# The compressed attention branch with both key groups in one TensorE product, padded to 128 rows

## The reference, cut to what matters

```python
s_c = jnp.einsum("bqgrd,bngd->bqgrn", qb, k_cmp) * scale     # n = 31 compressed keys, d = 64
m_c = (cmp_last[None, :] <= t[:, None])[None, :, None, None, :]
p_c, _, _ = _masked_softmax(s_c, m_c)
o_c = jnp.einsum("bqgrn,bngd->bqgrd", p_c.astype(qb.dtype), v_cmp)
...
return gb[..., 0:1] * o_c + gb[..., 1:2] * o_s + gb[..., 2:3] * o_w
```

## Time and profile before

| | before |
|---|---|
| median of 3 runs | 1529.16 us |
| lowest, highest of the 3 | 1528.4, 1537.82 us |
| the profiled execution's own time | 1526.18 us |
| span of the profiled execution | 1524.4 us |
| mean granted TensorE clock | 0.989 of full |
| TensorE matmul busy | 1455.0 us, 95% of the span |
| VectorE, ScalarE, GpSimd busy | 52%, 40%, 37% |

### The profile page before, as it was taken

How to read it: one execution, slowest core, us unless ns; L and a number is a source line. 1 busy time by engine, 2 the same in 40 slices (tenths; PEclk the granted TensorE clock), 3 DMA queues, 4 the chain that set the end, 5 groups by cost and what they waited for, 6 DMA issues and landing times.

```text
span 1524.4 us, 20393 instructions
## 1 busy us (share of the span) xinstructions
PE 1455.0 (95%) x7122; PEld 1140.8 (75%) x7122; DVE 790.8 (52%) x1413; ACT 605.0 (40%) x1104; POOL 569.4 (37%) x236
## 2 busy tenths in 40 slices
PE   6988999999999999789999999999999999999996
PEld 5656878888888888446778888888877777666785
DVE  6885542223444578895452223444477437676434
ACT  5443432232222436764432223222264335644432
POOL 3222354444444343211344444444434642222341
PEclk9999999999999999899999999999999999999998
DMA  5211222222222322100223222222214321111221
GB/s 215 73 56 51 97 97 96 96 96 97 96 96 96 97 84 83 55 29 29 69 83 96 96 96 98 97 96 97 97 66 126 124 97 56 56 56 56 70 69 55
DMA packets 36624, 129.55 MB, mean 85 GB/s; under 512 B 4048, under 2 KB 4176, under 8 KB 36560
## 3 DMA queue, kind: packets, MB, share of 16 engines
q1 hardware_dynamic: 35136, 124.80, 24.6%
q10 hardware_dynamic: 1424, 3.90, 0.7%
HBM read 126.58 MB, written 2.10 MB: 84 GB/s over the span
## 4 chain that ended last, share of the span: by engine, by line
PE 45%; issue 37%; POOL 14%; DVE 3%; ACT 1%; POOLq 0%; DVEq 0%; ACTq 0%
POOL w L627 14%; PE bank L644 13%; PE bank L646 13%; PE bank L645 13%; PE bank L769 2%; PE bank L783 2%; PE bank L749 1%; PE bank L1079 0%; DVE rms L1634 0%; DVE opC L1602 0%; PE bank L713 0%; DVE arena L2172 0%; DVE arena L2051 0%; PE bank L702 0%; DVE arena L1785 0%
## 5 line engine op out<-in xcount | busy, mean ns | idle before, releaser
L627 POOL TENSOR_TENSOR w<-raw,w 128x1024 fp32r<-128x1024 f32 x232 | 569.1, 2457 | 921.9 <-ACT w L1188 543.1
L644 PE MATMUL bank<-opC,w 128*128 128x512 f32 x624 | 253.5, 406 | 15.0 <-DVE opC L1602 10.5
L646 PE MATMUL bank<-opC,w 128*128 128x512 f32 x624 | 245.2, 393 | 0.0
L645 PE MATMUL bank<-opC,w 128*128 128x512 f32 x624 | 244.8, 392 | 0.0
L1761 DVE TENSOR_TENSOR mlp_op<-arena,mlp_op 128x512 fp32r<-128x512 f32 x64 | 144.5, 2260 | 188.7 <-ACT mlp_op L1303 188.7
L1275 ACT ACTIVATE w<-raw 128x1024 fp32r<-128x1024 f32 x126 | 133.2, 1057 | 239.5 <-PE bank L646 239.5
L644 PE MATMUL bank<-mlp_op,w 128*128 128x512 f32 x544 | 212.3, 390 | 3.1 <-ACT arena L1393 1.4
L646 PE MATMUL bank<-mlp_op,w 128*128 128x512 f32 x544 | 211.8, 389 | 0.0
L645 PE MATMUL bank<-mlp_op,w 128*128 128x512 f32 x544 | 211.8, 389 | 0.0
L644 PE MATMUL bank<-opA,w 128*128 128x512 f32 x416 | 162.8, 391 | 2.2 <-DVE arena L1756 1.3
L646 PE MATMUL bank<-opA,w 128*128 128x512 f32 x416 | 162.0, 389 | 0.0
(11 more groups left out here) (218 smaller groups left out, 1922.2 us busy)
## 6 DMA issues: line engine op xcount, KB each, us to landing
raw<-stream_dram SPq DMA_DIRECT2D x232, 512.0 KB, 3.4
out_t_dram<-arena SPq DMA_DIRECT2D x8, 256.0 KB, 2.2
x<-x_t_dram SPq DMA_DIRECT2D x4, 256.0 KB, 5.7
x<-x_t_dram ACTq DMA_DIRECT2D x4, 256.0 KB, 7.0
rope<-ropes_dram ACTq DMA_DIRECT2D x2, 512.0 KB, 6.8
con<-consts_dram ACTq DMA_DIRECT2D x1, 993.5 KB, 8.2
arena<-p_t_dram ACTq DMA_DIRECT2D x1, 512.0 KB, 3.7
par<-params_dram ACTq DMA_DIRECT2D x1, 253.5 KB, 3.8
```

The lines of the kernel that those rows point to most:

```text
L627: pool.tensor_tensor(w_lo[:, j, :], raw[:, j, :], w_hi[:, j, :].bitcast(F32), ALU.subtract).then_inc(lo_made, 1)
L644: pe.matmul(out, wh, hi, start=first, stop=False)
L645: pe.matmul(out, wh, lo, start=False, stop=False)
L646: return pe.matmul(out, wl, hi, start=False, stop=last)
```

## The change

For a compressed pair all three TensorE steps now treat both key groups at once.

- Scores: `cmpk` becomes 128 x 64 with the keys of group 0 in rows 0 to 63, columns 0 to 31, those of group 1 in rows 64 to 127, columns 32 to 63, and zeros elsewhere. One product with the whole 128 x 128 query tile gives 128 x 64 scores, both groups side by side in one PSUM bank. The 32nd column is now computed too and masked.
- Turn: the probabilities of both groups lie side by side in one buffer and are transposed at once into 64 rows. ScalarE copies them with one instruction in place of two.
- Values: `cmpv` becomes 128 x 128, with values of group 0 in rows 0 to 31, columns 0 to 63, of group 1 in rows 32 to 63, columns 64 to 127, and zeros elsewhere. One product contracts over 128 rows; the rows 64 to 127 of the moving operand hold what an earlier unit left there, and meet zeros.
- Preparation: two memsets on VectorE ahead of the last attention; `compressed` issues the value product twice, once per row block; the eviction takes four instructions in place of two.

```diff
-        cmpk = sb("cmpk", [P, 32])
-        cmpv = sb("cmpv", [32, P])
+        cmpk = sb("cmpk", [P, 64])
+        cmpv = sb("cmpv", [P, P])
...
-                n = N_CMP if br == 0 else P * (qt + 1)
+                n = 32 if br == 0 else P * (qt + 1)
...
+                q = z2(8 + u["r"])[:, P * qt:P * (qt + 1)]
+                return dict(qk=[(q, cmpk[:, :]) if br == 0 else (q[b, :], z2(11 + 2 * br)[b, 0:n])], n=n, both=br == 0,
...
-                            v=[cmpv[0:N_CMP, b]] if br == 0 else
+                            v=[cmpv[:, :]] if br == 0 else
...
+        def scores_of(units, i):
+            n = units[i]["n"]
+            return bank[2][:, n * (i % 2):n * (i % 2 + 1)] if both(units, i) else bank[2 + i % 2][:, 0:n]
+        def shares_of(units, i):
+            n = units[i]["n"]
+            return probs(i - i % 2, SEQ)[:, n * (i % 2):n * (i % 2 + 1)] if both(units, i) else probs(i, n)
...
+                    if both(units, 2 * p):
+                        pe.matmul(bank[2][:, 0:2 * units[2 * p]["n"]], *units[2 * p]["qk"][0], start=True,
+                                  stop=True).then_inc(s_full, 2)
+                        return
...
+                    if both(units, i):
+                        at, u = units[i]["out"][1], units[i]
+                        pe.matmul(into[:, at:at + P], u["v"][0], tmp[:, 4, 0:P], start=u["first"], stop=u["last"],
+                                  skip_group_check=True).then_inc(pv_done, 2)
+                        return
...
+                    if both(units, 2 * p):
+                        w = 2 * units[2 * p]["n"]
+                        pe.transpose(bank[4][0:w, 0:P], probs(2 * p, w), ident).then_inc(pt_full, 2)
+                        return
...
-                return pe.matmul(into[0:32, P:2 * P], hid[:, 1, :], g("w2v", 0, P), start=True, stop=True)
+                for at in (0, 32):
+                    mm = pe.matmul(into[at:at + 32, P:2 * P], hid[:, 1, :], g("w2v", 0, P), start=True, stop=True)
+                return mm
...
+                        if both(units, i):
+                            if i % 2 == 0:
+                                m = 2 * u["n"]
+                                nc.scalar.activation(tmp[0:m, 4, 0:P], bank[4][0:m, 0:P], ACT.Copy).then_inc(pt_ready, 2)
+                            continue
...
-                    mark(TS(cmpk[:, :], src[:, 0:32], 0.5, None, ALU.mult))
-                    TS(cmpv[:, :], src[0:32, P:2 * P], 0.5, None, ALU.mult).then_inc(z_ready, 1)
+                    mark(TS(cmpk[0:64, 0:32], src[0:64, 0:32], 0.5, None, ALU.mult))
+                    mark(TS(cmpk[64:P, 32:64], src[64:P, 0:32], 0.5, None, ALU.mult))
+                    mark(TS(cmpv[0:32, 0:64], src[0:32, P:P + 64], 0.5, None, ALU.mult))
+                    TS(cmpv[32:64, 64:P], src[32:64, P + 64:2 * P], 0.5, None, ALU.mult).then_inc(z_ready, 1)
...
+            mark(nc.vector.memset(cmpk[:, :], 0.0))
+            step(nc.vector.memset(cmpv[:, :], 0.0))
             attention("last", last_out, behind=behind_last)
```

More of the change, by code:

```diff
@@ L557, in unit @@
                 qt, br = u["qt"], u["branch"]
-                n = N_CMP if br == 0 else P * (qt + 1)
+                n = 32 if br == 0 else P * (qt + 1)
                 col = 32 * qt + 9 * u["g"] + 3 * u["r"] + br
-                return dict(qk=[(z2(8 + u["r"])[b, P * qt:P * (qt + 1)],
-                                 cmpk[b, 0:N_CMP] if br == 0 else z2(11 + 2 * br)[b, 0:n])], n=n,
-                            mask=c("cmpmask", 32 * qt, 32 * qt + N_CMP) if br == 0 else c("causal", 640 - n, 640),
+                q = z2(8 + u["r"])[:, P * qt:P * (qt + 1)]
+                return dict(qk=[(q, cmpk[:, :]) if br == 0 else (q[b, :], z2(11 + 2 * br)[b, 0:n])], n=n, both=br == 0,
+                            mask=c("cmpmask", 32 * qt, 32 * (qt + 1)) if br == 0 else c("causal", 640 - n, 640),
                             scale=HD ** -0.5, sink=None,
-                            v=[cmpv[0:N_CMP, b]] if br == 0 else
+                            v=[cmpv[:, :]] if br == 0 else
                               [z2(12 + 2 * br)[:, P * t + b.start:P * t + b.stop] for t in range(qt + 1)],
@@ L578, in program, with both @@
         GROUP0 = {"even": 0, "mla": 4}
+        def both(units, i):
+            return units[i].get("both", False)
+        def scores_of(units, i):
[4 more added lines that the diff above has]
+            return probs(i - i % 2, SEQ)[:, n * (i % 2):n * (i % 2 + 1)] if both(units, i) else probs(i, n)
         def out_bank(family, group):
@@ L1235, in exponentials @@
                         w = u["n"] + (u["sink"] is not None)
-                        nc.scalar.activation(probs(i, w), tmp[:, i % 2, 0:w], ACT.Exp, bias=negm[:, i:i + 1], scale=-1.0,
+                        nc.scalar.activation(shares_of(units, i) if both(units, i) else probs(i, w), tmp[:, i % 2, 0:w], ACT.Exp, bias=negm[:, i:i + 1], scale=-1.0,
                                              accum_out=den[:, i:i + 1]).then_inc(exp_done, 1)
@@ L1712, in reductions @@
                         nc.vector.tensor_tensor_reduce(
-                            tmp[:, i % 2, 0:u["n"]], bank[2 + i % 2][:, 0:u["n"]], u["mask"], -u["scale"],
+                            tmp[:, i % 2, 0:u["n"]], scores_of(units, i), u["mask"], -u["scale"],
                             3e38 if u["sink"] is None else col, ALU.add, ALU.min, negm[:, i:i + 1]).then_inc(masked, 1)
@@ L1723, in shares @@
                         dve.wait_ge(vstep, inverted[i % 2])
-                        pr = probs(i, u["n"])
+                        pr = shares_of(units, i)
                         if u["gate"] is None:
```

## The result

The change makes the kernel slower by 0.17%: 1531.47 us median (20 runs, 1528.8 to 1533.54) against 1528.46 (20 runs of the kernel before beside them), ratio 1.0017, 95% interval 1.0009 to 1.0025. The forecast was 1524.5 us, 0.3% faster, and its range ended at 1529.5. The profiled execution took 1529.27 us against 1526.18, with a mean granted clock of 0.985 against 0.989.

What follows compares the result with a forecast made beforehand. TensorE was taken as the bound, its matmuls covering 95% of the span. Scores and values 3.85 plus turn 1.1 less 0.3 added work gave 4.65 us off 1529.16: 1524.5 us; own range 1522.3 to 1526.2, overall 1521 to 1529.5.

Steps and rivals of the forecast that it cites:

- Scores and values: TensorE's compressed blocks in the last attention: ten records become six, 1.07 to 0.67 us each, 3.85 us saved in all.
- turn: Two 31-column transposes on TensorE become one of 64 columns: 11 x 0.10 = 1.1 us saved, alternatives 0 or 2.3.
- Rival (a): In padded TensorE records weights no longer load beside a matmul, 0.3 us more per block: 1527.3 us, chance 0.04.
- Absorbed blocks: Blocks of steps 24 and 39 only lengthen TensorE's waits in steps 25 and 40, so their 0.40 us each gives nothing.
- What it adds: Extra value product of `compressed` (0.15 us) and two more eviction pieces (0.17) lose 0.3 us, bounds 0.1 and 0.6; memsets hidden.
- Less work for ScalarE (12 copies): ScalarE's 12 fewer copies, like the extra softmax column, lie beside TensorE's stream and count 0.
- (b): The longer wait of step 25 makes TensorE's clock fall, costing 1.7 us: 1526.2 us, chance 0.11.
- (d): The clock falls from step 25 for 10.24 us, costing 5.1 us, slower than before: 1529.6 us, chance 0.04.
- (c): More TensorE waits on VectorE and ScalarE open, taking back four of eight blocks, 1.6 us: 1526.1 us, chance 0.13.

Runs made afterwards that it cites:

- e3: e1 with VectorE evacuating each dilated group's values ahead of the step's other work, not behind it: 1519.7 us, ratio 0.994.
- e1: The changed kernel, with ScalarE skipping the two leftover waits of a compressed pair's second unit: 1528.66 us, ratio 1.0004.
- e2: The kernel before with one more, long-met wait on ScalarE ahead of its wait for the sum of the exponentials: 1531.67 us, ratio 1.003.
- e5: The kernel before with VectorE evacuating each dilated group's values ahead of the step's other work: 1525.05 us, ratio 0.9978.
- e9: e1 with TensorE's filling products ahead of the values in steps 25, 35, 40 and 45: 1527.04 us, ratio 0.998.
- e4: The kernel before with the compressed keys and values evicted in four pieces in place of two, layout unchanged: 1530.19 us, ratio 1.0016.
- e6: The kernel before with only the compressed pairs' scores in one padded product, turns and values still in pieces: 1530.01 us, ratio 1.0004.
- e7: e1 with the padding for turn and values alone, scores made in two pieces as before: 1529.32 us, ratio 1.0.
- e10: e9 with VectorE also evacuating each dilated group's values ahead of the step's other work: 1521.25 us, ratio 0.9947; again 1520.21 us, 0.995.

## Why the prediction was wrong

**Scores and values, turn: right.** 0.66 us a block against 0.67, 0.11 a turn against 0.10. Within the block some luck: the scores take 0.16 and the values 0.28, where the sum had 0.22 for each. The term for both was 4.95 us; from step 12 to the normalisation e3 gains 4.83, net of a wait of step 25 that grew by 0.29 and one of step 40 that grew by 0.41. Rival (a) is refuted: two value records with 128 rows take 0.28 us up to the start of the turns, and the six records of the block 0.66, not 0.3 more. The rule of the Trainium skill (TensorE: Matmul & The Clock Gate, Part 3), that a load overlaps a running matmul only when the row group differs, doesn't hold for these records either: the six take 0.11 us each. The 64-column turn pays no pause, as the row of 31 columns had said; of the term's bounds, 0 and 2.3, neither came. The restriction in the Trainium skill, TensorEngine Tiling (Array Packing), Restrictions and Gotchas, that column tiling excludes the transpose mode for 32-bit input, fits the trace: the next product starts 0.05 us behind the 64-column turn.

**Absorbed blocks: about right.** The waits of steps 25 and 40 grew by 0.29 (e1) and 0.40 us, where I had 0.40 each.

**What it adds: 0.3 forecast, 0.65 measured.** The extra product of `compressed` costs TensorE nothing: its four records took 0.41 us (line 1069), as two did. The eviction was priced by two pieces' mean; it took 0.63 us more on VectorE, twice my upper bound of 0.30, and none of that was hidden. Nor were the memsets, held to be hidden, quite free (0.12 us at V4). The bound for the term, 0.6, was just passed.

**"Less work for ScalarE (12 copies), lie beside TensorE's stream: 0" failed.** I counted the instructions ScalarE loses and not the waits that stay behind when they go. One of them moved a table load of 1.28 us from under VectorE's work onto the path of step 25. It is worth 1.35 us by itself; with the half clock, the kernel before pays 3.0 us for it (e2). The view that would have shown it beforehand is ScalarE's timeline behind the copies: a load that is free only as long as no wait comes ahead of it.

**The clock, put at nothing in the forecast, failed as well, and the rivals (b) and (d) in their size and place.** I let the clock fall at one place, step 25, for 1.7 us or 5.1, from the point at which its idle piece reaches the 2.45 us of step 7; 0.15 for both together. The runs show it behind pieces of 1.89 (e5), 2.18 (e1) and 1.18 us and a second short wait behind it (step 40 of the changed kernel), at up to three places, 13.65 us of half clock in all. (d) had the right sign, at 1529.6, by luck: half of the clock's loss lies elsewhere, and the wait of step 25 was opened by the table load, not by the block. (c) didn't come: no wait but those of steps 25, 40 and 45 grew in e3. And the steps 35, 40 and 45 had no rival at all, although two of them were in my rows as waits.

**The account of the changed kernel**, from its marks and e3's: blocks and turns -5.6 us (the 4.83 of e3 and the 0.29, 0.41 and 0.07 by which its waits of steps 25, 40 and 45 grew); memsets and eviction +0.6; the longer wait of step 25 +1.65, of which the table load is 1.35; half clock behind it +2.7; behind steps 40 and 45 +1.7 and +1.6; longer waits of steps 40 and 45 +0.5: +3.15 us, against 3.16 measured. Without the bare wait the rest is about even with before (e1), and without the half clock the sum would be a gain, so it took both for the loss.

**The range.** Its own terms give 1525.9 us as the upper end of the forecast (1524.5 + 1.1 + 0.3), not 1526.2; the result lies above either.

**Open**: what decides whether an idle piece of about 2 us draws a stretch at half clock. The same piece of step 7, 2.45 us, did in before and did not in e9; that of step 25 with 2.18 us did in e1 and did not in e3, and with 1.89 us it did in e5 and did not in before and e4. Plainest is step 35: its two pieces, 1.38 or 1.39 and 0.56 us, are the same in before, after and e1 to e7, and a stretch at half clock follows in e1, e6 and e7 alone. What the traces show to differ is the place in time: 1315.48 (e1) and 1309.97 (e3) for the end of the piece in step 25. So a part of e3's gain, too, may be its place. An eviction in whole 128-row pieces, and the early evacuation with the bare wait left in, weren't tried.

## What to carry to other kernels

When an instruction is dropped and its waits are kept, look at what the orphaned wait now stands ahead of: here it cost 1.35 us by pushing a table load behind another engine's work. On an engine that is 95% busy a local gain can be forecast to a hundredth of a microsecond and still be worth nothing, since being earlier makes a wait further on longer (step 25 by 0.29 us, step 40 by 0.40), and the clock can fall behind it; so price every place at which that engine waits, and shorten these waits first (e5), then the gain arrives (e3). Compare two traces by starts counted from a mark that both share, with the granted clock beside it: the page's busy times, 1455.0 and 1455.1 us, said nothing.

## What was not expected of the hardware

A wait without an instruction held back a table load that the program writes behind it (1305.89 against 1307.98, lines 1522 and 1556). Short VectorE operations on 32 or 64 rows start 0.22 to 0.25 us apart when each begins at another row than the last, and 0.14 apart in e4, where the last two pieces read the same 32 rows; that the row is the cause isn't shown. Four matmul records into two row ranges of one bank took no longer than two (0.41 us, line 1069). And a stretch at half clock followed idle pieces of 1.2 to 2.5 us in some executions and not in others, though each kernel here that was profiled twice (after, e1, e10) had it at the same steps of the last attention both times, or, e10, at none.
